# Reordering the edges between the stages of a two-block fp32 transformer program

## The chip, the cores and the metric

The program runs on one core of one Trainium2 chip. A core has four compute engines with their own instruction queues: TensorE (PE: matrix products into PSUM), VectorE (DVE), ScalarE (ACT) and GpSimd (POOL). SyncE (SP) issues DMA transfers. The engines meet only through semaphores. The metric is the device time of one execution in microseconds (us).

## The reference

Two transformer blocks one after the other, on 256 tokens of width 2048, in float32. Cut to what matters here:

```
# block 1
x = x + mixed(rms_norm(x, g_mix)) @ w_out      # 16 heads: 6 differential, 4 block, 6 dilated
x = x + cross_attention(rms_norm(x), rms_norm(mem))          # w_cq, w_ckv, w_co
x = x + (silu(conv(h @ w_up_g)) * (h @ w_up_u)) @ w_down     # h = rms_norm(x), width 5632
x = rms_norm(x, g_final)
# block 2
h = h + 0.5 * rmsnorm(swiglu(rmsnorm(h)))                    # ff1
o_attn = nsa_attention(...)                                  # 8 heads
log_a = -8 * sigmoid(xc @ w_a + b_a) * softplus(-lam); a = exp(log_a)
u = sqrt(1 - exp(2 * log_a)) * (sigmoid(xc @ w_i + b_i) * xc)
o_rec = scan(a, u) * gelu(yb)                                # h_t = a_t h_(t-1) + u_t
h = h + rmsnorm(concat(rmsnorm(o_attn), rmsnorm(o_rec)) @ w_out)
h = h + 0.5 * rmsnorm(swiglu(rmsnorm(h)))                    # ff2
h = h + rmsnorm(sigmoid(rmsnorm(h) @ w_ple_gate) * (p @ w_ple_proj))
```

## The kernel before

**Data and precision.** Activations lie transposed: 128 features on the partitions, 256 tokens along the free dimension, so width 2048 is 16 chunks. X holds the residual stream. Every float32 product is made of three faster ones. Weights and operands are split into a high part and a low part (value minus high part), and hi*hi, hi*lo and lo*hi are added in PSUM. OPR and HR hold operand chunks as (high, low) pairs.

**Units.** The weights (about 590 MB) stream once. SyncE loads a unit of 256 x 512 weights (512 KB) into one of four slots of `raw` (L450). ScalarE copies it to `wh` (`split`, L1061), VectorE subtracts to get `wl` (`split`, L1583), TensorE multiplies. `LEAD` is 4: each engine issues the split of unit n+4 at its place for unit n, and ScalarE's split waits until TensorE has used the slot. In `gemm` (TensorE, L575 on) a unit is 16 matmuls: for each of two chunks and four output tiles one of 512 columns (high weights times high and low operand, L610 or L615) and one of 256 (low weights times high operand, L612). In `unit` (L640 on; matmuls L648, L650, L651), used for w_in_b, w_out, nsa, wo_a and wo_r, it is 24 matmuls of 256 columns.

**Phases** run in the order of the list PHASES: w_in, w_in_b, w_out, w_ck, w_cq, w_cv, w_co, up, down, ff1_up, ff1_down, in_c, nsa, wo_a, wo_r, ff2_up, ff2_down, ple_gate, ple_p, ple_gb, ple_pl. A column block of 512 outputs takes 4 PSUM banks, and blocks alternate between the two halves of PSUM. At its end ScalarE copies the half of the sum that came from the low operand (`take`, L1079), VectorE adds the other (`collect`, L1597) and frees the banks (`acc_free`); `residual` then adds to X (L1690). In four phases (PAIRED: up, ff1_up, ff2_up, ple_gate) the first two column blocks run interleaved, so each pair of operand chunks serves two units.

**Norms.** Before a norm's first product the operand is the un-normalised x times the gain: ScalarE writes the high part (L1162), VectorE the low part (`prep`, L1754), chunk by chunk. The sum of squares is folded on VectorE (`fold`, L1709 to L1718), summed over partitions by TensorE with a matrix of ones (`stat` L538, `late_stat` L573, `post_stat` L561), rooted on ScalarE (`std`, L1147) and inverted on VectorE (`rstd`, L1725). The scale is applied at evacuation. Norms behind a phase (`post_stat`, `post_norm`) must be complete before the next one starts; `post_norm` then updates X (L1779 and L1781 for the single chunks 0 to 3, L1786 and L1791 for groups of four). Meanwhile TensorE runs filler matmuls whose result nobody reads (`keep_busy`, L548): 8 and then 20, none at ple_post.

**Order written by hand.** Each engine's program is a straight list of steps. In w_in_b and w_out 88 steps interleave units with the heads of attention: step s on TensorE is unit s and then pieces of heads. The unit order of w_out is OUT_UNITS, pairs of column block c and weight rows r; rows 3 and 4 need the four heads that finish last (head outputs L1875). In nsa 84 steps do the same with eight heads whose scores stand at steps 50, 54, ... 78 (NSTART), the rotary turns (TURNS_OF_ROPE, products L937, VectorE `rotate` L2141), and two units of recurrent gates, ("r", 0) and ("r", 1), at steps 75 and 77 (`gate_pairs`, L865 to L867). A gate unit has four pairs of PSUM tiles in three banks, so its fourth pair waits for ScalarE's first sigmoid (`gate_sigmoids`, L1435). The exponentials of a head are `n_exp` (L1408). The gate scaling is VectorE's L2277. The recurrence (`recurrence(n)` on VectorE, L2290 to L2306, and ScalarE's L1508 to L1519) is interleaved with the 16 units of wo_a: product ig*xc (L2290), exp, tanh, exp, sqrt, product (L2297), eight scans (L2301), product with gelu (L2306).

Two places in which an engine's order decides, of ScalarE from L1444 on:

```
for s in range(84):
    if s in (75, 77):
        gate_sigmoids((75, 77).index(s), (0, 1, 2))
    if s > 0:
        split(n0 + s + LEAD, 0)
```

and of TensorE's wait for two chunks per unit: `lambda u: pe.wait_ge(xs_lo, first + per_unit * (u + 1))`.

GpSimd does the sums of squares of the norms behind a phase and of mem, attn and rec (`squares`, L2445 to L2448), each norm in its order, and nothing else. At the end VectorE updates X in four groups of four chunks, and SyncE stores each group (L527).

## Time and profile before

| | us |
|---|---|
| median of 3 runs | 3328.53 (3327.95 to 3330.65) |
| the profiled execution | 3328.18 |
| its span, first to last instruction | 3325.9 |
| mean granted TensorE clock | 0.993 |
| bytes moved by DMA | 595.78 MB, 179 GB/s on average |

The profiled execution's own time is 2.3 us longer than its span. The table of a profile's busy times says how long each engine had an instruction at work. The table of waits says, for each line, how long the engine stood idle before it and which instruction of which engine came last before it went on. A window adds up busy times in a stretch and shows the clock granted to TensorE (1.00 is 2.4 GHz, 0.50 is 1.2 GHz). A timeline lists instructions in order: start, duration, engine, line, operation, output <- inputs, shapes, and in brackets the idle time before.

### The profile page before, as it was taken

How to read it: one execution, taken by the hardware profiler on the slowest of the kernel's cores; microseconds unless marked ns; L12 is line 12 of the kernel's file. 1: busy time of each engine (PE TensorE's matmuls, PEld its weight loads, DVE VectorE, ACT ScalarE, POOL GpSimd, SP SyncE). 2: the span in 40 equal slices, each digit the busy share in tenths (PEclk: the TensorE clock that was granted, in tenths of full speed). 3: DMA queues.
4: the chain of work that ended last, by engine and by line, in shares of the span. 5: the costliest groups of instructions: out<-in, count | busy, mean ns of one | idle time of the engine just before them, and what ended most of it. 6: DMA issues, size and time to landing. Idle time of an engine off the chain costs nothing.

```text
span 3325.9 us, 51311 instructions
## 1 busy us (share of the span) xinstructions
PE 3252.5 (98%) x19952; PEld 2889.8 (87%) x19952; DVE 2102.9 (63%) x2273; ACT 1581.0 (48%) x1886; POOL 91.0 (3%) x38
## 2 busy tenths in 40 slices
PE   8999999999999999999999998999999999999997
PEld 7999987888888888888888887998988888888886
DVE  6676676766665546665565547756886555555477
ACT  5445455554454435444444434445644444444353
POOL 0000200000000100000000000000010000000001
PEclk9999999999999999999999999999999999999998
DMA  7555555666666555656656564754456566565543
GB/s 254 178 153 168 168 177 152 184 189 190 188 180 196 187 190 161 193 181 194 187 184 194 185 191 136 216 152 121 159 159 196 183 191 187 178 200 184 193 159 126
DMA packets 321867, 595.78 MB, mean 179 GB/s; under 512 B 18276, under 2 KB 41988, under 8 KB 321732
## 3 DMA queue, kind: packets, MB, share of 16 engines
q1 hardware_dynamic: 313856, 587.27, 56.7%
q10 hardware_dynamic: 7876, 6.63, 0.6%
q8 instruction: 93, 1.52, 0.2%
q14 instruction: 42, 0.34, 0.0%
HBM read 591.70 MB, written 2.13 MB: 179 GB/s over the span
## 4 chain that ended last, share of the span: by engine, by line
PE 94%; DVE 3%; ACT 1%; issue 1%; POOL 0%; DMA 0%; ACTq 0%; DVEq 0%; POOLq 0%
PE acc L610 26%; PE acc L612 25%; PE acc L615 24%; PE acc L648 5%; PE acc L650 5%; PE acc L651 5%; DVE wl L1583 1%; ACT wh L1061 0%; DVE RSTD L1725 0%; DVE T L1786 0%; PE acc L561 0%; PE acc L665 0%; PE acc L844 0%; PE acc L845 0%; PE acc L846 0%
## 5 line engine op out<-in xcount | busy, mean ns | idle before, releaser
L1583 DVE TENSOR_TENSOR wl<-raw,wh 128x1024 fp32r<-128x1024 f32 x1112 | 1388.1, 1257 | 1037.0 <-ACT wh L1061 1035.9
L1061 ACT ACTIVATE wh<-raw 128x1024 fp32r<-128x1024 f32 x1112 | 1165.9, 1057 | 1319.4 <-PE acc L615 1047.3
L612 PEld LDWEIGHTS acc<-OPR,wl 128*128 128x128 f32 x4992 | 940.8, 188 | 207.2
L610 PE MATMUL acc<-OPR,wh 128*128 128x512 f32 x2658 | 1041.7, 397 | 17.9 <-DVE OPR L1754 11.8
L612 PE MATMUL acc<-OPR,wl 128*128 128x256 f32 x4992 | 1011.3, 279 | 0.0
L615 PE MATMUL acc<-OPR,wh 128*128 128x512 f32 x2334 | 924.6, 396 | 0.0
L610 PEld LDWEIGHTS acc<-OPR,wh 128*128 128x128 f32 x2658 | 505.9, 190 | 38.4 <-issue 10.2
L612 PEld LDWEIGHTS acc<-HR,wl 128*128 128x128 f32 x2208 | 414.9, 188 | 95.0
L610 PE MATMUL acc<-HR,wh 128*128 128x512 f32 x1138 | 447.1, 396 | 1.0 <-DVE HF L1597 1.0
L612 PE MATMUL acc<-HR,wl 128*128 128x256 f32 x2208 | 439.7, 278 | 0.0
L615 PEld LDWEIGHTS acc<-OPR,wh 128*128 128x128 f32 x2334 | 438.2, 188 | 0.0
L615 PE MATMUL acc<-HR,wh 128*128 128x512 f32 x1070 | 423.3, 396 | 0.0
L648 PE MATMUL acc<-OPR,wh 128*128 128x256 f32 x1216 | 350.4, 288 | 2.9 <-DVE wl L1583 2.9
L650 PE MATMUL acc<-OPR,wh 128*128 128x256 f32 x1216 | 344.5, 283 | 0.0
L651 PE MATMUL acc<-OPR,wl 128*128 128x256 f32 x1216 | 344.4, 283 | 0.0
L648 PEld LDWEIGHTS acc<-OPR,wh 128*128 128x128 f32 x1216 | 233.6, 192 | 8.1 <-issue 7.9
L650 PEld LDWEIGHTS acc<-OPR,wh 128*128 128x128 f32 x1216 | 233.7, 192 | 0.9 <-issue 0.7
L651 PEld LDWEIGHTS acc<-OPR,wl 128*128 128x128 f32 x1216 | 233.5, 192 | 0.0
L610 PEld LDWEIGHTS acc<-HR,wh 128*128 128x128 f32 x1138 | 215.9, 190 | 4.8 <-DVE HF L1597 1.6
L615 PEld LDWEIGHTS acc<-HR,wh 128*128 128x128 f32 x1070 | 200.5, 187 | 0.0
L1079 ACT ACTIVATE T<-acc 128x1024 f32<-128x1024 f32 x94 | 95.0, 1010 | 17.7 <-PE acc L615 16.3
L1597 DVE TENSOR_TENSOR T<-acc,T 128x1024 f32<-128x1024 f32 x78 | 95.1, 1219 | 1.0 <-ACT T L1079 1.0
(346 smaller groups left out, 2008.2 us busy)
## 6 DMA issues: line engine op xcount, KB each, us to landing
raw<-in_w_up SPq DMA_DIRECT2D x176, 512.0 KB, 4.4
raw<-in_ff_w_gate SPq DMA_DIRECT2D x176, 512.0 KB, 3.8
raw<-in_ff_w_up SPq DMA_DIRECT2D x176, 512.0 KB, 4.4
raw<-in_ff_w_down SPq DMA_DIRECT2D x176, 512.0 KB, 3.8
raw<-in_w_in SPq DMA_DIRECT2D x170, 512.0 KB, 3.9
raw<-in_w_down SPq DMA_DIRECT2D x88, 512.0 KB, 4.0
raw<-in_w_out SPq DMA_DIRECT2D x64, 512.0 KB, 3.8
raw<-in_w_ple_gate SPq DMA_DIRECT2D x32, 512.0 KB, 3.9
```

The costliest lines, as they stand in the source:

```text
L610: pe.matmul(acc[:, b + t, :], wh[:, s, col:col + P], x, start=first, stop=False)
L612: mm = pe.matmul(acc[:, b + t, 0:T], wl[:, s, col:col + P], x[:, 0, :], start=False, stop=last and t % 2 == 0)
L615: mm = pe.matmul(acc[:, b + t, :], wh[:, s, col:col + P], x, start=False, stop=last)
L648: pe.matmul(dst, w_hi, ks[k][:, 0, :], start=first and k == 0 and t % 2 == 0, stop=False, skip_group_check=True)
L650: pe.matmul(dst, w_hi, ks[k][:, 1, :], start=False, stop=False, skip_group_check=True)
L651: mm = pe.matmul(dst, w_lo, ks[k][:, 0, :], start=False, stop=last and k == 1, skip_group_check=True)
L1061: act.activation(wh[:, s, :], raw[:, s, :], ACT.Copy).then_inc(hi_done, 1)
L1079: act.activation(T1[:, 0:tiles, :], acc[:, b:b + tiles, T:2 * T], ACT.Copy).then_inc(t1_full, 1)
L1583: dve.tensor_tensor(wl[:, s, :], raw[:, s, :], wh[:, s, :].bitcast(F32), ALU.subtract)\
L1597: dve.tensor_tensor(dst, acc[:, b:b + tiles, 0:T], T1[:, 0:tiles, :], ALU.add).then_inc(acc_free, 1)
```

## The change

TensorE's program:
- The bias-table product (L634) moves behind unit 3 of w_in.
- In w_in the late statistic comes behind unit 2 of block 1, not unit 1.
- A paired phase waits for the last evacuation (`acc_free`) only at its second unit; in up, ff1_up, ff2_up and ple_gate its first unit waits chunk by chunk.
- In w_out the last units of blocks 0 and 1 are ordered rows 3, 3, 4, 4; rows 3 wait for 11 parts, not 13.
- TensorE waits for the root of the memory statistic behind w_out's last unit, not at once.
- One rotary turn moves from step 55 to 56. The recurrent gates move to steps 79 and 81. TensorE waits for the last sigmoid before wo_a. The attention statistic comes behind unit 2 of wo_a, not unit 3.
- At ple_post 12 filler matmuls run.

ScalarE and VectorE: the last split of w_cv moves behind the head outputs, the last split of w_co behind the residual. The updates of the first chunks are reordered around the operands. Gate scaling moves to steps 82 and 83. A small sigmoid stands ahead of the gates at step 79. The functions of the recurrence come one step earlier; A's exponential stands ahead of `std("attn")`. The product ig*xc goes from VectorE to GpSimd, behind the attention squares. At the end ScalarE multiplies the output by its gain into YG, the fold of ple_post comes earlier, and VectorE updates five groups (4, 4, 4, 2, 2 chunks), each stored by itself.

```diff
@@ lists
-             + [(0, 3), (0, 4), (1, 3), (1, 4)] + ...
+             + [(0, 3), (1, 3), (0, 4), (1, 4)] + ...
-    return units + rec[:25] + [("r", 0), rec[25], ("r", 1)] + rec[26:]
+    return units + rec[:29] + [("r", 0), rec[29], ("r", 1)] + rec[30:]
-TURNS_OF_ROPE = {..., 53: (5, 4, 7), 55: (6, 6, 7)}
+TURNS_OF_ROPE = {..., 53: (5, 4, 7), 56: (6, 6, 7)}
+OUT_GROUPS = [(0, 4), (4, 8), (8, 12), (12, 14), (14, 16)]
+        YG = HFc[:, 52:68, :]
@@ sync
-            for g in range(4):
-                sp.wait_ge(out_done, g + 1)
+            for n, (first, last) in enumerate(OUT_GROUPS):
+                sp.wait_ge(out_done, n + 1)
...
@@ tensor, post_stat
-                if name != "ple_post":
-                    keep_busy(name, 8)
+                keep_busy(name, 12 if name == "ple_post" else 8)
@@ tensor, gemm
-                    if paired:
-                        pe.wait_ge(acc_free, g)
-                    elif g >= 2:
+                    if g >= 2:
                         pe.wait_ge(acc_free, i * 2 + (g - 1))
...
-                        ready(u)
+                        if paired and v == 1:
+                            pe.wait_ge(acc_free, g)
+                        if half is None or v > 0 or not paired:
+                            ready(u)
                         pe.wait_ge(lo_done, i * (2 * ph["upc"]) + (n + 1))
                         for k in range(chunks):
+                            if half is not None and v == 0 and paired:
+                                pe.wait_ge(xs_lo, half + k + 1)
...
+                        if g == 0 and u == 3:
+                            pe.wait_ge(tab_loaded, 48)
+                            pe.matmul(acc[0:16, 2, :], HF[0:32, 0:16], HF[0:32, 512:1024], start=True, stop=True)\
+                              .then_inc(rt_ps, 1)
...
-                        if norm and isinstance(i, int) and c == late and u == 1:
+                        if norm and isinstance(i, int) and c == late and u == (2 if name == "w_in" else 1):
@@ tensor, w_out
-                first, last = s in (0, 6, 16, 24), s in (13, 15, 23, 31)
+                first, last = s in (0, 6, 16, 24), s in (14, 15, 23, 31)
-                pe.wait_ge(xs_lo, XS["attn1"] + (13 if r in (3, 4) else 9 if r >= 5 else 3))
+                pe.wait_ge(xs_lo, XS["attn1"] + (13 if r == 4 else 11 if r == 3 else 9 if r >= 5 else 3))
-                    stat("mem", colsum)
+                    stat("mem", colsum, wait=False)
+            pe.wait_ge(var_ready, N["mem"] + 1)
@@ tensor, wo_a
+            pe.wait_ge(r_sig, 8)
-                if n == 3:
+                if n == 2:
                     stat("attn", colsum, wait=False)
@@ scalar and vector, w_cv and w_co
-                split(PH["w_cv"]["u0"] + u + LEAD, 0)
+                if u < 7:
+                    split(PH["w_cv"]["u0"] + u + LEAD, 0)
...
+            split(PH["w_cv"]["u0"] + 7 + LEAD, 0)
-                splits(ph, c, 0)
+                splits(ph, c, 0, 0, 1 if c == 3 else 2)
...
+            splits(ph, 3, 0, 1)
@@ scalar, nsa and wo_a
-                if s in (75, 77):
-                    gate_sigmoids((75, 77).index(s), (0, 1, 2))
+                if s == 79:
+                    act.activation(SM[:, 62:63], SM[:, 60:61], ACT.Sigmoid)
+                if s in (79, 81):
+                    gate_sigmoids((79, 81).index(s), (0, 1, 2))
-                if n == 3:
-                    std("attn", 1024)
-                if n == 3:
+                if n == 2:
                     act.wait_ge(r_la, 1)
                     act.wait_ge(units_used, n0 + 84)
                     act.activation(A_, LA, ACT.Exp).then_inc(r_a, 1)
+                    std("attn", 1024)
...
@@ scalar, end
+            def scale_y(g):
+                act.wait_ge(y_done, g + 1)
+                for c in range(4 * g, 4 * g + 4):
+                    ins = act.activation(YG[:, c, :], HFc[:, 20 + c, :], ACT.Copy, scale=v("ple_post_g_2", c))
+                ins.then_inc(y_scaled, 1)
...
@@ vector, prep of the first chunks
                     if update and c == 0:
                         update(0, 0)
-                    if update and c < 3:
-                        update(0, c + 1)
+                        update(0, 1)
+                    elif update and c == 2:
+                        update(0, 3)
...
                     if c == 1 and sq in FIRST_X:
+                        update(0, 2)
                         split(ph["u0"] + 3, 0)
@@ vector, nsa and wo_a
-                if s in (80, 82):
+                if s in (82, 83):
...
-                if n == 2:
-                    dve.wait_ge(r_sig, 8)
-                    dve.tensor_tensor(IX, IX, XC, ALU.mult).then_inc(r_ix, 1)
-                if n == 5:
+                if n == 4:
                     dve.wait_ge(r_a, 3)
                     dve.scalar_tensor_tensor(LA, LA, 1.0, XC, ALU.add, ALU.mult).then_inc(r_w, 1)
-                if n == 7:
+                if n == 6:
...
-                if n in (8, 9):
+                for c in {7: (0, 1), 8: (2, 3, 4), 9: (5, 6, 7)}.get(n, ()):
...
@@ vector, end
+            early_fold("ple_post")
             collect(gb, 1, 0, gate(3))
             collected(gb, 1, 0)
             apply_rstd(3)
-            early_fold("ple_post")
...
+            for n, (first, last) in enumerate(OUT_GROUPS):
+                k = last - first
+                dve.wait_ge(y_scaled, first // 4 + 1)
+                if n >= 1:
+                    dve.wait_ge(out_done, n)
+                chain(dve.tensor_tensor(T2[:, 0:k, :], YG[:, first:last, :], bc(RSTD[:, :], k), ALU.mult))
+                dve.tensor_tensor(X[:, first:last, :], X[:, first:last, :], T2[:, 0:k, :], ALU.add).then_inc(out_done, 1)
@@ gpsimd
             squares("attn", four(HFc, OF, 1), n_of, 8, 0)
+            gp.wait_ge(r_sig, 8)
+            gp.wait_ge(xc_lo, 8)
+            gp.tensor_tensor(IX, IX, XC, ALU.mult).then_inc(r_ix, 1)
```

## Rows read from the trace of the kernel before

**Rows 1.** The page, first part: busy us (share of the span) xinstructions of each engine.

```profile
PE 3252.5 (98%) x19952; PEld 2889.8 (87%) x19952; DVE 2102.9 (63%) x2273; ACT 1581.0 (48%) x1886; POOL 91.0 (3%) x38
```

**Rows 2.** Waits of TensorE: line <- releaser: us in total, times, longest.

```profile
PE acc L610 <- DVE OPR L1754: 11.8, 7, 2.9
PE acc L634 <- DMA HF<-in_diag: 9.9, 1, 9.9
PE acc L865 <- ACT HF L1435: 4.9, 1, 4.9
PE acc L610 <- DVE T L1597: 4.4, 1, 4.4
PE acc L648 <- DVE wl L1583: 2.9, 3, 2.2
PE acc L573 <- issue: 2.9, 2, 2.3
PE acc L779 <- DVE HF L1979: 2.7, 1, 2.7
...
PE acc L648 <- ACT S L1147: 2.6, 1, 2.6
PE acc L648 <- DVE HR L1875: 2.4, 1, 2.4
...
PE acc L937 <- DVE S L2141: 1.4, 1, 1.4
```

**Rows 3.** Windows: length, busy us (x) of PE PEld DVE ACT POOL, PEclk, DMA.

```profile
363.50:366.90 3.40, 3.40 (x18) 3.40 (x18) 0.00 (x0) 0.04 (x1) 3.24 (x3) 0.50 0.39 136
407.90:411.30 3.40, 3.40 (x18) 3.40 (x17) 1.16 (x1) 0.00 (x0) 0.00 (x0) 0.50 0.47 149
532.60:537.60 5.00, 5.00 (x16) 4.32 (x17) 1.98 (x3) 0.19 (x1) 0.00 (x0) 0.50 0.31 103
600.00:650.00 50.00, 50.00 (x289) 43.58 (x288) 33.71 (x34) 25.43 (x28) 0.00 (x0) 1.00 0.69 210
2308.10:2312.50 4.40, 4.36 (x20) 4.36 (x21) 1.23 (x1) 3.24 (x7) 0.00 (x0) 0.50 0.00 0
2338.70:2353.40 14.70, 14.68 (x121) 14.46 (x120) 13.52 (x19) 6.22 (x9) 1.93 (x1) 1.00 0.45 147
```

**Rows 4.** Timeline of VectorE at the edge of w_co and up: start, us, instruction.

```profile
531.31 1.22 DVE L1597 TENSOR_TENSOR T<-acc,T 128x1024 f32<-128x1024 f32 x1
```

**Rows 5.** Timeline of VectorE at the start of ff2_up.

```profile
2449.16 0.48 DVE L1754 SCALAR_TENSOR_TENSOR OPR<-X,vec,OPR 128x256 fp32r<-128x256 f32 x1
...
2450.41 0.48 DVE L1754 SCALAR_TENSOR_TENSOR OPR<-X,vec,OPR 128x256 fp32r<-128x256 f32 x1
```

**Rows 6.** Timeline of VectorE and TensorE around the attention statistic in wo_a.

```profile
2348.82 1.23 DVE L1583 TENSOR_TENSOR wl<-raw,wh 128x1024 fp32r<-128x1024 f32 x1 [1.08 <-ACT wh L1061]
2349.96 1.22 DVE L1709 TENSOR_TENSOR T<-HF 128x1024 f32<-128x1024 f32 x1
...
2353.68 0.70 PE L538 MATMUL acc<-S,ones 128*128 128x256 f32 x2 [0.30 <-DVE S L1718]
```

**Rows 7.** Timeline of GpSimd and VectorE where both work, and the product that moves.

```profile
366.24 2.39 POOL L2448 TENSOR_TENSOR S<-S 128x1024 f32<-128x1024 f32 x1
...
367.95 1.76 DVE L1583 TENSOR_TENSOR wl<-raw,wh 128x1024 fp32r<-128x1024 f32 x1 [5.75 <-ACT wh L1061]
...
2354.68 2.28 DVE L2290 TENSOR_TENSOR HF<-HF 128x2048 f32<-128x2048 f32 x1
```

**Rows 8.** Timeline of ScalarE before the recurrent gates' first sigmoid.

```profile
2305.96 1.28 ACT L1435 ACT_TABLE_LOAD   x1
```

**Rows 9.** Timeline of TensorE and VectorE at the end of the program.

```profile
3305.08 3.34 PE L561 MATMUL acc<-S,ones 128*128 128x256 f32 x8 [1.42 <-ACT S L1114]
...
3319.65 1.67 DVE L1786 SCALAR_TENSOR_TENSOR T<-HF,vec,RSTD 128x256 f32<-128x256 f32 x4
3321.36 1.22 DVE L1791 TENSOR_TENSOR X<-X,T 128x1024 f32<-128x1024 f32 x1
```

81 lines of the change are left out of this document (44 added, 37 removed).

## The prediction

> **What bounds the kernel now.** I read four views, in this order. The page's first part shows TensorE busy for 98% of the span [rows 1], and nearly all of that is matrix work which the change leaves alone. A gain can come from only two things: time in which TensorE stands still, and time in which it works at its lower clock. So I then read the table of TensorE's waits [rows 2], which names each standstill and the instruction that ended it. Third, windows laid over the stretches behind the longer waits: the granted clock there is 0.50, which is 1.2 GHz in place of 2.4, and TensorE works on through them [rows 3]. Every us at half clock costs half a us. Last, timelines of VectorE, ScalarE and GpSimd around each edge, to see what is late next once a wait goes [rows 4 to 9].
>
> The waits shown sum to about 46 us. The last matmuls end at 3308.4 [rows 9], 17.5 before the end of the span. The four slow stretches shown cost half of 16.2, about 8. The page shows no other loss, so the change must be added up edge by edge. A unit of 16 matmuls takes 2.8 us (289 in 50), one of 24 takes 2.9 (120 in 14.7) [rows 3].
>
> **The change part by part.** Gains carry a minus sign.
>
> *Start.* The bias-table product (L634) leaves the head of TensorE's queue, where it waited 9.9 us for its DMA [rows 2]. The first unit then waits for its own split, ready at the same time, and runs its 1.8 us earlier, but at half clock. That is worth 0.9, and the product, at full clock by then, costs about 0.9 behind unit 3. Sum 0, between -1 and +0.5.
>
> *w_in, second column block.* TensorE waited 2.3 of the 2.9 us at L573 for the column sums [rows 2]. The statistic now comes one unit later, and a unit of 2.8 us fills the wait. The split of unit 13 has one unit less in hand; I estimate that half a us is left, and 0.8 would come back if it is late. **-2.3**.
>
> *w_out.* The units of rows 3 are done before those of rows 4, each waiting only for its own heads. The 2.4 us at L648 <- HR L1875 goes [rows 2], and with it the 3.4 us at half clock right behind [rows 3], worth 1.7. The evacuation of block 0 moves from step 14 to 15 and is needed one unit of 2.9 us later; it takes as long as other additions of its size, 1.2 [rows 4]. **-4.1**.
>
> *Statistic of the memory.* TensorE no longer waits for ScalarE's root at L648 <- S L1147, 2.6 us, and the 3.4 us at half clock behind it lose their cause [rows 2, 3]. The root still blocks ScalarE, but a split is due three units after its slot is free: 8.7, less 1.1 and 1.2 for its two halves, leaves 6. **-4.3**.
>
> *w_cv to w_co.* One split moves behind the value evacuation. The wait of 2.7 us [rows 2] was ended by VectorE, which did that split first. What is late next is ScalarE's own evacuation behind its last copy. I take half, with 0 and 2.7 as bounds. **-1.4**.
>
> *w_co to up.* One split moves behind the last residual, and the first unit of up no longer waits for the last evacuation, which reads other banks. The wait of 4.4 us goes [rows 2]. The second unit still needs that evacuation: a copy of 1.0 and an addition of 1.2 [rows 4], behind one split and two operand halves on a packed VectorE; I make that 3.1 us against a unit of 2.8, so 0.3 comes back. Of the slow stretch behind, 5 us were worked [rows 3], worth 2.5. **-6.6**.
>
> *Rope.* One rotation moves from step 55 to 56; the 1.4 us at L937 goes [rows 2]. **-1.4**.
>
> *Waits per chunk in ff1, ff2 and ple.* Seven waits at L610 <- OPR L1754 make 11.8 us [rows 2]. In ff2 the first two chunks were ready at 2449.64 and 2450.89, the ends of the two L1754 rows [rows 5]. Starting on the first saves 1.25, in ple as much. In ff1 I take 0.4, since there the filler matmuls outlast the first chunk. Three of the seven waits, in the column block in_c, are VectorE's pace: there the reordered updates only add a wait for ScalarE's copy, +0.3. Behind ple_gate VectorE's chain can follow only in part, +0.4. **-2.2**.
>
> *End.* The sums of squares are folded before the last collection, so VectorE is 1.1 us freer when it matters. Twelve filler matmuls keep TensorE going: the eight statistic matmuls took 3.34 us at half clock [rows 9] and would take about half. ScalarE's table load of 1.28 [rows 8] becomes the later partner, so I make the reciprocal 1.3 earlier, not 1.7. Then four times a multiplication of 1.67 (4 instructions) and an addition of 1.22 [rows 9] become five pairs of plain VectorE operations at 1.22 for four chunks [rows 4] and 0.7 for two (an estimate, a little over half): about 10.3 against 11.8. ScalarE's scaling of groups 0 and 1 fits between its splits (it is 48% busy [rows 1]), that of 2 and 3 beside the reciprocal; a group late would cost up to 1.7. The last store is half as large: -0.3. **-3.1**.
>
> These sum to **-25.4**.
>
> *The recurrent branch* is where I expect a loss.
> - The gates move from steps 75 and 77 to 79 and 81. TensorE's 4.9 us at L865 [rows 2] came because ScalarE, in order, first did the exponentials of the head of step 74, then a table load of 1.28 [rows 8], then the sigmoid. Step 79 stands just so behind the head of step 78. The new dummy sigmoid stands behind the exponentials too, so it hides nothing. The wait stays, and so do the 4.4 slow us behind it [rows 3]. **+0.2** for the dummy.
> - The attention statistic moves from unit 3 to unit 2 of wo_a, but VectorE's fold stays behind its split of unit 1, which waits for TensorE. The fold began at 2349.96, and the statistic of 2353.68 waited 0.30 for its end, behind unit 3 [rows 6]. Unit 2 ends a unit of 2.9 earlier. So TensorE waits 3.2 where it waited 0.3: **+2.9**.
> - The product of 2048 columns, 2.28 on VectorE [rows 7], goes to GpSimd, in just this stretch. GpSimd needed 2.39 for 1024 columns of two sources, and a split which VectorE began meanwhile took 1.76 and ended only after GpSimd did [rows 7]; the usual split takes 1.23 [rows 6]. So VectorE stands still for about 4.8. It has 1.08 idle before the fold [rows 6], and four gate scalings move in too (about 1 overlapped; at 0.48 each [rows 5] 1.9). Operand halves for units 1 and 2 and the fold come 4.6 later. **+4.6**.
> - Freed of that product and with scans one step earlier, VectorE no longer delays three splits at the end of wo_a, 2.9 us [rows 2]. **-2.9**.
> - The chain through ScalarE and the scans now starts later. Its last product, then the operands of wo_r and the second fold, come about 2.4 after TensorE wants them. **+2.4**.
> - A wait of nearly 4 us may lower the clock once more, 1.7; I take half. **+0.9**.
>
> Sum **+8.1**, between 0 (VectorE and GpSimd side by side, chain in time) and +13 (GpSimd a third slower, two slow stretches).
>
> On GpSimd the row shows a split held until the other engine was done [rows 7]. The Trainium skill says the same in "SBUF — State Buffer", section "Who interferes with whom": a VectorE instruction with two SBUF inputs contends with a GpSimd instruction that reads SBUF, and the later one blocks fully. By that rule the term is 4.6; if the two only shared the port it would be near 2.
>
> A table load takes 1.28 in the row, with the next activation right behind it [rows 8]. The Trainium skill, "ScalarE: Activation LUTs", section "What ACT_TABLE_LOAD costs", gives about 2.7 with a drain for a change of set. The change adds one such load in wo_a; by that figure my sum would be an estimated 1.4 higher.
>
> Total: -25.4 + 8.1 = -17.3. The profiled execution took 3328.18 (span 3325.9), 0.35 below the median of the three runs, so 3310.9 on its own terms and about **3311** as a median.
>
> **The rivals.**
> - *The recurrent branch costs nothing.* For it: GpSimd's spans are rough, and VectorE is freed where it was late. Against it: the fold's order, which no other engine can shorten. With the branch at +1.5 the time is 3304.5. Chance 0.21.
> - *The gate wait goes.* The step's surroundings differ (no convolution work near step 79), so ScalarE may be free before. Then 4.9 and 2.2 less: about 3304. Against it: ScalarE's order is written out. Chance 0.09.
> - *Freed time is lost again.* TensorE arrives sooner at places paced by VectorE or by loads, and a third to a half of the 18 us won before up comes back as new waits. For it: VectorE's operand halves already hold TensorE seven times [rows 2]. Against it: between w_in and down nearly all VectorE work starts on TensorE's signals. About 3319. Chance 0.12.
> - *Slower.* Place: the 32 units of wo_a and wo_r. New waits at units 1, 2 and the statistic keep the clock at 1.2 GHz, so each unit of 2.9 us takes 5.8. It makes the kernel slower by over 0.2% once 17.3 + 6.7 = 24 us are eaten, which is after 8 to 9 slow units; all 32 would give 3311 + 92, about 3400. Against it: no slow stretch in rows 3 outlasts 7 us, after waits up to 4.9. Chance 0.03.
>
> My own account has 0.55.
>
> **How the numbers follow.** 0.2% of this time is 6.7 us, about what a measurement can tell from no change. The forecast with the bounds of its unknown terms reaches from 3305 to 3319, the first two rivals lie at 3304, the third at 3319. The range 3302 to 3319.5 leaves out less than 2 in 10. Faster by over 0.2% means below 3321.9: 0.55, 0.21, 0.09 and most of 0.12, less something for what I have not seen, 0.92. Within 0.2%: 0.05. Slower: 0.03.
>
> **What would show each step right or wrong.** In the waits after: no rows for w_out, memory or rope, L573 down to about half a us, and the residual wait at up near 0.3. The wait at L865 still near 5 with a table load before it. A wait of 3 to 4 us at L538 behind VectorE's L1718 analogue, and waits at L648 on operand halves in the first two units of wo_a. VectorE splits or scalings of over 3 us beside a GpSimd product of about 4.8. Fewer slow stretches before 600 us. I am wrong if the statistic's wait is under 1, if VectorE runs on beside GpSimd, or if waits before up return elsewhere.

## The result, and the profile after

The changed kernel takes **3308.77 us** (median of 4 runs, 3308.55 to 3310.74). The kernel before took 3329.18 beside it (median of 4, 3327.95 to 3330.65). The ratio is 0.9944, with a 95% interval of 0.9931 to 0.9956: 18.6 us faster, 14.6 to 23.0 (the two medians as they stand are 20.4 apart). The forecast was 3311.0, with a range from 3302 to 3319.5. The spans of the two profiled executions are 3325.9 and 3306.7, so the traces have 19.2 us to account for.

The page's first part, of the kernel after:

```profile
PE 3250.7 (98%) x19964; PEld 2889.8 (87%) x19964; DVE 2105.9 (64%) x2263; ACT 1587.6 (48%) x1903; POOL 97.5 (3%) x39
```

TensorE's busy time fell by 1.8 us [rows 1]; the rest of the 19.2 is standstill and the tail behind the last matmul. TensorE's waits after, whole span (line <- what ended the wait: us in total, times, longest):

```profile
PE acc L616 <- DVE wl L1610: 11.8, 2, 10.0
PE acc L616 <- DVE OPR L1782: 6.9, 5, 2.8
PE acc L874 <- ACT HF L1448: 5.6, 2, 5.0
PE acc L542 <- DVE S L1745: 3.2, 1, 3.2
PE acc L656 <- DVE OPR L2252: 2.4, 1, 2.4
PE acc L542 <- issue: 1.6, 1, 1.6
...
PE acc L788 <- DVE HF L2009: 1.3, 1, 1.3
PE acc L576 <- issue: 1.1, 1, 1.1
```

Lines have moved: L616 is the L610 of before, L656 is L648, L874 is L865, L542 is L538, L788 is L779, L576 is L573, L1610 is the split L1583, L1782 is L1754, L1745 is L1718. Compare with [rows 2]. In the first row 10.0 us are the first unit's wait for its own split, where the bias-table product waited 9.9 before. Gone are the waits of w_out (2.4), of the memory's root (2.6), of the residual ahead of up (4.4, of which 0.3 is left) and of the rotation (1.4), and at the end of wo_a those for VectorE's splits (2.9). The waits for operand halves at a stage's start (L1754, now L1782) went from seven with 11.8 us to five with 6.9, all in in_c. New in wo_a and wo_r are the statistic (3.2), operand halves (2.4), 0.8 at the operands of wo_r and 1.6 at the second statistic. L576 shows 1.1, not the half a us that I had named as a sign; it is all in in_c. The gate wait stands as it was, 5.0, with 0.6 more in the second gate unit.

Both programs have the same 1112 splits on ScalarE, one for each weight unit, so the n-th split serves as a milestone. Its start, in us:

| up to split | what lies before it | before | after | difference | of this stretch | forecast |
|---|---|---|---|---|---|---|
| 61 | start, w_in | 185.63 | 183.46 | -2.17 | -2.2 | 0, -2.3 |
| 123 | w_out | 395.79 | 389.44 | -6.35 | -4.2 | -4.1 |
| 146 | memory | 465.96 | 455.30 | -10.66 | -4.3 | -4.3 |
| 160 | w_cv to w_co | 517.08 | 505.03 | -12.05 | -1.4 | -1.4 |
| 301 | w_co to up | 919.87 | 901.48 | -18.39 | -6.3 | -6.6 |
| 651 | ff1 | 1907.15 | 1888.08 | -19.07 | -0.7 | -0.4 |
| 751 | in_c | 2197.41 | 2177.57 | -19.84 | -0.8 | +0.3 |
| 816 | rope, recurrent branch | 2449.70 | 2436.39 | -13.31 | +6.5 | -1.4 + 8.1 |
| 1001 | ff2 | 2968.07 | 2953.42 | -14.65 | -1.3 | -1.25 |
| 1091 | ple_gate | 3229.72 | 3213.76 | -15.96 | -1.3 | -1.25 |
| 1112 | ple_gb | 3290.00 | 3273.98 | -16.02 | -0.1 | +0.4 |
| end of span | end | 3325.9 | 3306.7 | -19.2 | -3.2 | -3.1 |

The shape is the forecast one: about 21 us are won up to the gates, 7.9 are lost between them and the end of wo_r, and some 6 are won behind. Up to 600 us [rows 3] has three low-clock windows. The first two lines below are about the same microseconds of w_out after the change, the other three are the low-clock windows around the recurrent branch (length, busy us (x) of PE, PEld, DVE, ACT, POOL, then the granted clock):

```profile
363.00:366.90 3.90, 3.90 (x35) 3.90 (x34) 1.99 (x3) 1.56 (x2) 3.82 (x2) 1.00 0.44 140
407.00:411.30 4.30, 4.30 (x38) 4.30 (x37) 1.41 (x2) 2.12 (x2) 0.00 (x0) 1.00 0.54 161
2302.70:2306.10 3.40, 2.87 (x13) 2.87 (x14) 0.03 (x1) 3.06 (x8) 0.00 (x0) 0.50 0.00 1
2326.60:2330.00 3.40, 3.40 (x18) 3.40 (x18) 3.40 (x8) 0.00 (x0) 0.00 (x0) 0.50 0.10 25
2336.80:2340.20 3.40, 3.35 (x13) 3.18 (x14) 1.12 (x1) 2.93 (x3) 0.00 (x0) 0.50 0.32 100
```

No low-clock window is left between 16 and 600 us. Around the branch there are three of 3.4 us, where one of 6.8 stood.

### The profile page after: what moved, and what is told of

Its sections match the earlier page's. It is cut to its first block, busy times and chain, and to the rows that moved or that the text cites. A ratio compares the mean times of both kernels' runs of the same rounds, so it can differ in the third digit from the quotient of the medians.

```text
span 3306.7 us, 51352 instructions
## 1 busy us (share of the span) xinstructions
PE 3250.7 (98%) x19964; PEld 2889.8 (87%) x19964; DVE 2105.9 (64%) x2263; ACT 1587.6 (48%) x1903; POOL 97.5 (3%) x39
## 4 chain that ended last, share of the span: by engine, by line
PE 95%; DVE 3%; ACT 1%; issue 1%; POOL 0%; DMA 0%; ACTq 0%; DVEq 0%; POOLq 0%
PE acc L616 26%; PE acc L618 25%; PE acc L621 24%; PE acc L656 5%; PE acc L658 5%; PE acc L659 5%; DVE wl L1610 1%; PE acc L552 1%; ACT wh L1071 0%; PE acc L673 0%; DVE HF L2309 0%; PE acc L853 0%; PE acc L854 0%; PE acc L855 0%; PE acc L760 0%
## 5 line engine op out<-in xcount | busy, mean ns | idle before, releaser
L1610 DVE TENSOR_TENSOR wl<-raw,wh 128x1024 fp32r<-128x1024 f32 x1112 | 1385.0, 1255 | 1013.8 <-ACT wh L1071 1012.4
L616 PE MATMUL acc<-OPR,wh 128*128 128x512 f32 x2658 | 1040.5, 397 | 19.2 <-DVE wl L1610 11.8
L616 PEld LDWEIGHTS acc<-OPR,wh 128*128 128x128 f32 x2658 | 505.2, 190 | 38.4 <-issue 14.3
L616 PE MATMUL acc<-HR,wh 128*128 128x512 f32 x1138 | 447.1, 396 | 1.0 <-DVE HF L1624 1.0
L656 PE MATMUL acc<-OPR,wh 128*128 128x256 f32 x1216 | 351.6, 289 | 3.7 <-DVE OPR L2252 2.4
L656 PEld LDWEIGHTS acc<-OPR,wh 128*128 128x128 f32 x1216 | 234.5, 193 | 9.0 <-issue 5.4
L616 PEld LDWEIGHTS acc<-HR,wh 128*128 128x128 f32 x1138 | 215.9, 190 | 4.8 <-DVE HF L1624 1.6
L1371 ACT ACTIVATE HR<-T 128x1024 f32 (+1 forms) x33 | 35.0, 1061 | 127.3 <-DVE T L2082 122.5
```

The lines of the kernel that those rows point to most:

```text
L616: pe.matmul(acc[:, b + t, :], wh[:, s, col:col + P], x, start=first, stop=False)
L656: pe.matmul(dst, w_hi, ks[k][:, 0, :], start=first and k == 0 and t % 2 == 0, stop=False, skip_group_check=True)
L1371: act.activation(HR[:, bass.ds(i * 4 + 4 * j, 4), 0, :], T2[:, :, :], ACT.Copy).then_inc(hid_hi, 1)
L1610: dve.tensor_tensor(wl[:, s, :], raw[:, s, :], wh[:, s, :].bitcast(F32), ALU.subtract)\
```

## The experiments

Every kernel ran beside the kernel before on the same chip; the first four below share a chip, the next three and the one with early edges undone a second, the spread scans and the two on the clock a third, and the one with the old order of the updates ran on a fourth. Medians are of 4 to 7 runs. The repeats of one kernel lie within 1 to 4 us, and the stretch up to split 61, which has the same code in all of them, alone moves a span by 1 us (the difference there is -2.2 after, but -2.2 to -3.2 in the experiments). So where less than 2 us matter I compare the traces, milestone by milestone.

The milestones vary too, with the place and length of the slow stretches. The last three kernels below have the changed kernel's code between splits 751 and 816. It loses 6.5 there, and they lose 7.4 (no matmuls ahead of the last statistic), 6.7 (early edges undone) and 7.4 (old order of the updates). In the two with 7.4 the gate wait of 5.0 us is followed by 6.8 us at half clock in place of 3.4. So a difference of under 1 us in this stretch says nothing, unless the slow stretches are alike. The window of the first of the three:

```profile
2300.50:2307.30 6.80, 4.83 (x22) 4.83 (x23) 2.63 (x8) 5.16 (x11) 0.00 (x0) 0.50 0.18 60
```

### Is the branch the loss?

**Branch back.** Gates, product, statistic and the steps of the recurrence as before, all else as after.

```diff
-    return units + rec[:29] + [("r", 0), rec[29], ("r", 1)] + rec[30:]
+    return units + rec[:25] + [("r", 0), rec[25], ("r", 1)] + rec[26:]
-                if s == 79:
-                    act.activation(SM[:, 62:63], SM[:, 60:61], ACT.Sigmoid)
-                if s in (79, 81):
+                if s in (75, 77):
...
+                if n == 2:
+                    dve.wait_ge(r_sig, 8)
+                    dve.tensor_tensor(IX, IX, XC, ALU.mult).then_inc(r_ix, 1)
```

> The changed kernel with the whole recurrent branch as it was before: gates at steps 75 and 77, the product on VectorE in unit 2 of wo_a, the attention statistic behind unit 3, its root, exponentials, scans and products one step later. Everything else of the change stays. My theory, that the branch costs time: in the two traces the distance between the kernels shrinks from about 21.6 us (behind the rope) to 13.3 us (end of wo_r), so this kernel should come out 8.3 us under the changed one, near 3300.5. In its trace the wait at the gate matmuls is about 4.9 and the statistic of the attention waits 0.3 or a little more. Rival, that the distance shrinks because TensorE arrives earlier at places that VectorE or the loads pace, whatever the branch does: then this kernel stays within 2 us of 3308.8 and the same waits stand in wo_a.

Measured: 3300.79 us, ratio 0.9918 (0.9905 to 0.9932). TensorE's waits from 2280 to 2440 us:

```profile
PE acc L874 <- ACT HF L1447: 4.9, 1, 4.9
PE acc L656 <- DVE wl L1607: 2.9, 3, 2.2
PE acc L564 <- ACT S L1123: 0.5, 1, 0.5
PE acc L542 <- DVE S L1742: 0.3, 1, 0.3
```

These are the waits of before. Between splits 751 and 816 this kernel gains 1.0 (-20.9 and -21.9 against the kernel before) where the changed one loses 6.5. So the branch costs 7.5 us, or 8.3 when this kernel is set against the two that have 6.8 slow us behind the gates, as it has. The gain of 1.0 is smaller than the rotation's 1.4 because 3.4 us at half clock follow the wait of 2.2 here (at 2368.3); the kernel before has that wait, but not the stretch.

**Product on VectorE again**, alone:

```diff
-            gp.wait_ge(r_sig, 8)
-            gp.wait_ge(xc_lo, 8)
-            gp.tensor_tensor(IX, IX, XC, ALU.mult).then_inc(r_ix, 1)
@@ vector, recurrence
+                if n == 2:
+                    dve.wait_ge(r_sig, 8)
+                    dve.tensor_tensor(IX, IX, XC, ALU.mult).then_inc(r_ix, 1)
```

> The changed kernel with only the product of input gate and convolution (2048 columns) back on VectorE, in unit 2 of wo_a. My theory: the scaling of 256 columns that took 4.69 us beside GpSimd's product takes 0.34 again, so the operand halves of units 0 and 1 are in time and the wait of 2.4 us at the head of wo_a goes with its slow stretch (1.7), while the statistic, which still follows VectorE's fold behind the split of unit 1, goes on waiting 2.5 to 3.3 us. About 3304.7. Rival, the held VectorE was waiting anyway and nothing else was due: 3308.8, and the 2.4 us stay or turn up at the fold. Second rival, the product's 2.28 us on VectorE is missed later in wo_a: between 3307 and 3309.

Measured: 3306.99 us, ratio 0.9934 (0.9921 to 0.9948), span 3304.7. Between splits 751 and 816 it loses 4.7 where the changed kernel loses 6.5: 1.8 less. The timeline of GpSimd in the changed kernel, then that of VectorE there (start, duration):

```profile
2318.30 1.92 POOL L2481 TENSOR_TENSOR S<-HF 128x1024 f32<-128x1024 f32 x1 [368.45 <-ACT HF L1436]
2320.19 4.65 POOL L2501 TENSOR_TENSOR HF<-HF 128x2048 f32<-128x2048 f32 x1
```

```profile
2318.13 7.12 DVE L2309 TENSOR_SCALAR HF<-HF,SM 128x256 f32<-128x256 f32 x4
2325.17 0.87 DVE L2252 SCALAR_TENSOR_TENSOR OPR<-HF,vec,OPR 128x256 fp32r<-128x256 f32 x2
```

And VectorE with the product back:

```profile
2319.20 2.77 DVE L2309 TENSOR_SCALAR HF<-HF,SM 128x256 f32<-128x256 f32 x4
2321.89 0.87 DVE L2252 SCALAR_TENSOR_TENSOR OPR<-HF,vec,OPR 128x256 fp32r<-128x256 f32 x2
```

The same four scalings take 7.12 us beside the 4.65 us product and 2.77 without it; in both, one of the four takes 1.99 beside GpSimd's squares. The row at L656 <- L2252 (2.4) is gone, as expected, and the statistic still waits 3.2. The slow stretches did not get fewer: two of 3.4 turned into one of 6.8, and the one behind the gate wait, in code that both kernels share, is 6.8 here and 3.4 in the changed kernel. Against the two kernels where it is 6.8 as well, 2.7 are saved. So the mechanism is as I said, and its price here is 1.8 to 2.7, not 4.

**Statistic behind unit 3 again**, alone:

```diff
-                if n == 2:
+                if n == 3:
                     stat("attn", colsum, wait=False)
@@ scalar, behind the exponential of A in step 2
-                    std("attn", 1024)
                 if n == 3:
+                    std("attn", 1024)
@@ vector
-                if n == 3:
+                if n == 4:
                     rstd("attn")
```

> The changed kernel with only the attention statistic behind unit 3 of wo_a again, the root and the reciprocal one step later with it. My theory: the statistic's wait of 3.25 us falls to 0.3 or so, since a unit of 2.9 lies before it, and the 3.4 us at half clock behind it lose their cause (1.7): about 3304.5. Rival, VectorE is late as a whole in wo_a and the wait only moves to the next place that needs it (the end of the first column block, or the operands of wo_r): within 1 us of 3308.8.

Measured: 3307.89 us, ratio 0.9939 (0.9926 to 0.9953), span 3306.3. The rival holds. TensorE's waits in the same stretch:

```profile
PE acc L656 <- DVE HF L2346: 4.2, 1, 4.2
PE acc L656 <- DVE OPR L2252: 2.4, 1, 2.4
...
PE acc L542 <- DVE S L1745: 0.4, 1, 0.4
```

The statistic waits 0.4 in place of 3.2, and the evacuation of the first column block (L2346) 4.2 in place of 0.5. What holds it is seen in ScalarE's timeline and then VectorE's:

```profile
2339.23 1.28 ACT L1157 ACT_TABLE_LOAD   x1
2340.52 0.47 ACT L1157 ACTIVATE S<-acc,SM 128x256 f32<-128x256 f32 x1
2341.01 1.28 ACT L1525 ACT_TABLE_LOAD   x1
2342.31 1.92 ACT L1525 ACTIVATE HF<-HF 128x2048 f32<-128x2048 f32 x1
2344.26 1.92 ACT L1527 ACTIVATE HF<-HF 128x2048 f32<-128x2048 f32 x1
2346.08 1.99 ACT L1071 ACTIVATE wh<-raw 128x1024 fp32r<-128x1024 f32 x2
```

```profile
2347.15 1.23 DVE L1610 TENSOR_TENSOR wl<-raw,wh 128x1024 fp32r<-128x1024 f32 x1 [6.68 <-ACT wh L1071]
2348.29 1.75 DVE L1752 RECIPROCAL RSTD<-S 128x256 f32<-128x256 f32 x1
2350.07 2.29 DVE L2322 SCALAR_TENSOR_TENSOR HF<-HF 128x2048 f32<-128x2048 f32 x1
2352.28 1.22 DVE L2346 TENSOR_TENSOR HF<-acc,RSTD 128x1024 f32<-128x1024 f32 x1
```

ScalarE does the root and two functions of 2048 columns, with two table loads, before its next split. VectorE idles 6.68 us for that split, then does the reciprocal and the 2.29 us product of the recurrence, and only then the evacuation. One step earlier in the recurrence means ahead of the evacuation.

**First gates at step 77**, second at 81, no extra sigmoid:

```diff
-    return units + rec[:29] + [("r", 0), rec[29], ("r", 1)] + rec[30:]
+    return units + rec[:27] + [("r", 0)] + rec[27:30] + [("r", 1)] + rec[30:]
...
-                    gate_sigmoids((79, 81).index(s), (0, 1, 2))
+                    gate_sigmoids((77, 81).index(s), (0, 1, 2))
...
```

> The changed kernel with the first set of gate matmuls and its sigmoids at step 77, between the exponentials of the heads at steps 74 and 78, and the second set left at 81; the extra sigmoid that only loads the table is dropped. My theory: TensorE's 5.0 us in the first set come from ScalarE doing the exponentials of the head just before, and at step 77 ScalarE is free, so the wait goes to under 1 us and with it the slow stretch behind (1.7): 3302 to 3303. Rival, the wait is the price of the four banks and the sigmoids themselves wherever they stand: a wait of 3 us or more is left at the gate matmuls. Second rival, the 6 us are given back in wo_a, where VectorE and GpSimd then have less time: 3306 to 3308, with longer waits on operand halves.

Measured: 3304.97 us, ratio 0.9930 (0.9917 to 0.9944). The waits for the sigmoids fall from 5.6 to 3.3 in all (1.2 and 2.0), each behind a table load; no slow stretch follows them, and the rows of wo_a are those of the changed kernel. Between splits 751 and 816 the kernel loses 2.9 where the changed one loses 6.5: 3.7 less. The profile has a slow stretch of 3.4 at 580 us which neither kernel has (+1.6), and the one in in_c falls where nothing hides it (+1.0, more on that below), so its span, 3304.8, is high by 2.5. The median lies between my theory (3302 to 3303) and the second rival. The first rival, 3 us or more wherever the gates stand, fell: in the unit that moved, the wait went from 5.0 to 1.2. The wait was ScalarE's exponentials, less the loads.

### Which part of the branch?

**Only the gates moved**, and **the same with the product on GpSimd**. In both the statistic is behind unit 3 again and the recurrence one step later, as before the change; the first also has the product on VectorE. Against the changed kernel:

```diff
@@ scalar: exponential, tanh, root, gelu of the recurrence one step later; std("attn") ahead of the exponential
@@ vector, recurrence
-                if n == 4:
+                if n == 5:
                     dve.wait_ge(r_a, 3)
-                if n == 6:
+                if n == 7:
                     dve.wait_ge(r_sw, 1)
-                for c in {7: (0, 1), 8: (2, 3, 4), 9: (5, 6, 7)}.get(n, ()):
+                if n in (8, 9):
```

> Of the recurrent branch only the gates stay moved (steps 79 and 81, their scalings at 82 and 83, the extra sigmoid); the product is back on VectorE, the attention statistic behind unit 3, and the root, exponentials, scans and products one step later, as before the change. The kernel with the whole branch back took 3300.8. My theory now: what cost 7.5 us in the branch is not the place of the gates (their two waits are 5.0 and 0.6, against 4.9) but what was moved inside wo_a: the product (2.0 measured alone) and VectorE's product of 2048 columns one step earlier, ahead of the evacuation of the first column block, where it waits for ScalarE. So 3301.5, between 3300.5 and 3303, with no wait on the evacuation in wo_a. Rival, the late gates themselves push VectorE's fold and operand halves back: 3304 or more, with a wait of over 2 us at the head of wo_a or at the statistic.

Measured: 3302.23 us, ratio 0.9926 (0.9912 to 0.9939), span 3299.6 against 3298.1 with the branch back. The gate waits are 5.6, and the other rows are again those of before (2.9, 0.5, 0.3). Between splits 751 and 816 it is 1.2 us behind that run, with slow stretches of the same lengths behind the same waits: the price of the late gates.

> As the run with only the gates moved, but the product of 2048 columns stays on GpSimd. My theory: the same as that run plus the 2.4 us at the head of wo_a (operand halves behind the scaling that GpSimd holds up) and perhaps one slow stretch (1.7): 3304 to 3305.6, and the wait of 4.2 us on the evacuation of the first column block, which stood in the run with only the statistic moved back, is gone since VectorE's long product stands behind that evacuation again. Rival, that wait came from the held VectorE and not from the order: then it is still there at 4 us and the time is 3307 to 3309.

Measured: 3306.01 us, ratio 0.9937 (0.9923 to 0.9951), 3.8 over the run without GpSimd's product on the same chip. The waits:

```profile
PE acc L874 <- ACT HF L1448: 5.6, 2, 5.0
PE acc L656 <- DVE OPR L2252: 3.4, 2, 2.4
PE acc L656 <- DVE wl L1610: 2.6, 2, 2.2
PE acc L542 <- DVE S L1745: 0.6, 1, 0.6
```

No wait on the evacuation: it came from the order, not from the held VectorE. And with the recurrence at its old place the product on GpSimd costs 3.8 (4.1 between the splits, the slow stretches alike), more than the same edit is worth in the changed kernel (1.8 to 2.7). The parts of the branch don't add: taken back one by one they give 1.8 to 2.7 and 0.5, the gates cost 1.2, and all together are 7.5 to 8.3. That they fall due behind each other on the same VectorE is my reading of the waits; no run tests it by itself.

**Both gates between two heads.** The branch as before, gates at 77 and 78, the one-column sigmoid at 76:

```diff
+    return units + rec[:27] + [("r", 0), ("r", 1)] + rec[27:]
+                if s == 76:
+                    act.activation(SM[:, 62:63], SM[:, 60:61], ACT.Sigmoid)
+                if s in (77, 78):
+                    gate_sigmoids((77, 78).index(s), (0, 1, 2))
```

> All of the branch as before the change, but the two gate units stand at steps 77 and 78, both between the exponentials of the heads at 74 and 78, and a one-column sigmoid at step 76 loads the table ahead of them; scalings at 80 and 82. My theory: the 4.9 us at the gates and the slow stretch of 6.8 behind it (3.4) go, since ScalarE is idle there: 3300.8 - 8 = 3293, and 1 us more if the fourth pair of each unit still waits for a sigmoid: 3292.5 to 3294.5. Rival, the second unit directly behind the first needs four banks that are not yet read, and the exponentials at 78 come late behind eight sigmoids: waits of 3 us are left and the time is 3296 to 3298.

Measured: **3296.67 us**, ratio 0.9908 (0.9893 to 0.9924), 12 under the changed kernel. The waits, then ScalarE's timeline there:

```profile
PE acc L656 <- DVE wl L1610: 2.9, 3, 2.2
PE acc L874 <- ACT HF L1448: 1.9, 2, 1.2
```

```profile
2285.50 1.28 ACT L1459 ACT_TABLE_LOAD   x1
2286.79 0.20 ACT L1459 ACTIVATE SM<-SM 128x1 f32<-128x1 f32 x1
2286.90 1.04 ACT L1071 ACTIVATE wh<-raw 128x1024 fp32r<-128x1024 f32 x1
2287.85 2.28 ACT L1448 ACTIVATE HF<-acc,vec 128x256 f32<-128x256 f32 x6
```

Between splits 751 and 816 it gains 5.5 us, the run with the branch back 1.0: 4.6 for the gates, where I expected 8. The time is the rival's (3296 to 3298), though 1.9 us of waits are left, not 3. Waits make 3.0 of the 4.6. The load starts at 2285.5, when TensorE is already at the gate unit, because ScalarE did the exponentials of step 74 and a split until then; so the load isn't hidden, and 1.2 of the first wait stays. And I had booked 3.4 for the slow stretch of 6.8. In the run with the branch back its window reads:

```profile
2283.00:2289.70 6.70, 3.89 (x18) 3.89 (x19) 2.72 (x9) 5.96 (x14) 0.00 (x0) 0.50 0.27 78
```

TensorE is busy for 3.89 of the 6.70 us; the rest is the wait itself. So the half clock cost at most half of 3.89, 1.9 and not 3.4; the 4.6 less the 3.0 of waits leave 1.6.

**Spreading the scans** on top of it:

```diff
-                if n in (8, 9):
-                    for c in range(4 * (n - 8), 4 * (n - 8) + 4):
+                for c in {7: (0, 1), 8: (2, 3, 4), 9: (5, 6, 7)}.get(n, ()):
```

> The kernel with the gates at steps 77 and 78 (3296.7), and from the change inside wo_a only the spreading: two scans in step 7, three each in 8 and 9, and the last product in two halves in steps 10 and 11; everything else in wo_a at its place of before. My theory: VectorE has 0.8 us idle behind its product in step 7, so two scans there cost nothing and take 1.3 us out of steps 8 and 9; the waits for VectorE's splits at the end of wo_a (0.36, 0.36, 2.2) fall to 1 us or less in all, and the slow stretch of 3.4 behind them (1.7) may go: 3293.5, between 3292.5 and 3296. Rival, the operands of wo_r, which need the last product, become the wait instead, now 1 us at the head of wo_r: 3296 to 3298.

Measured: **3296.12 us**, ratio 0.9902 (0.9887 to 0.9917), span 0.6 less than the run before it. VectorE's splits are in time (2.9 to 0.6), but 1.7 and 1.6 us turn up at the operands of wo_r and its statistic, which the changed kernel has too (0.8 and 1.6). The slow stretch behind them is gone. So the rival holds: the wait moved to wo_r. This is the fastest version I have: it beats the kernel before by some 33 us and the changed one by 12.6, but not measurably the one without the spreading.

### The clock

**A wait filled with matmuls.** The changed kernel, and ahead of the attention statistic:

```diff
                 if n == 2:
+                    for _ in range(13):
+                        pe.matmul(acc[:, 7, :], OPR[:, 8, 0, 0:P], OPR[:, 8, :, :], start=True, stop=True)
                     stat("attn", colsum, wait=False)
```

> The changed kernel with 13 matmuls of 512 columns, whose result nobody reads, ahead of the attention statistic, in the place where TensorE waits 3.25 us for VectorE's fold. At 0.23 us each they take 3.0. My theory, that a slow stretch follows a standstill: the wait shrinks to about 0.3 and the 3.4 us at half clock that follow it are not there, which is worth 1.7: 3307.1, with one slow stretch in wo_a (behind the operand halves) instead of two. Rival, the clock goes down for another reason than the standstill itself: the stretch is still there and the time is 3308.8 or a little more.

Measured: 3307.80 us, ratio 0.9938 (0.9924 to 0.9952), span 3305.0, 1.7 less. The wait at L542 is 0.3, and the window that stood at 0.50 now reads:

```profile
2336.80:2340.20 3.40, 3.40 (x28) 3.35 (x29) 0.94 (x1) 2.76 (x3) 0.00 (x0) 1.00 0.34 108
```

28 matmuls in place of 13. The slow stretch followed from the standstill: filled, it is gone, and between splits 751 and 816 that is worth 1.5, a little under half the stretch's length.

**No matmuls ahead of the last statistic:**

```diff
-                keep_busy(name, 12 if name == "ple_post" else 8)
+                if name != "ple_post":
+                    keep_busy(name, 8)
```

> The changed kernel without the twelve matmuls that keep TensorE busy ahead of the last statistic. My theory: TensorE stands still for 3 us or more behind the last column block, the eight statistic matmuls run at half clock again and take 3.3 us in place of 2.4, and everything behind them comes 0.8 to 1.5 us later: 3309.6 to 3310.3. Rival, the eight are paced by ScalarE's squares and its table load, which ends 0.1 us after them: under 0.5 us, not to be seen in the time.

Measured: 3309.45 us, ratio 0.9942 (0.9928 to 0.9955), span 3307.2. The eight statistic matmuls after, and in this run:

```profile
3288.62 2.40 PE L564 MATMUL acc<-S,ones 128*128 128x256 f32 x8 [0.37 <-ACT S L1124]
```

```profile
3288.63 2.93 PE L565 MATMUL acc<-S,ones 128*128 128x256 f32 x8 [3.14 <-ACT S L1125]
```

0.53 more, of which the span shows 0.5: nearly the rival. The last four wait for ScalarE's second square, and ScalarE's table load ends only 0.1 behind the eight in the changed kernel.

### The edges before and behind

**Early edges undone** in the changed kernel: w_out's order, the memory's root, and whole units again in up, ff1, ff2 and ple_gate:

```diff
-             + [(0, 3), (1, 3), (0, 4), (1, 4)] + ...
+             + [(0, 3), (0, 4), (1, 3), (1, 4)] + ...
-                    stat("mem", colsum, wait=False)
-            pe.wait_ge(var_ready, N["mem"] + 1)
+                    stat("mem", colsum)
-            gemm("up", *from_op(XS["ffn"]), half=XS["ffn"], norm="ffn")
+            gemm("up", *from_op(XS["ffn"]), norm="ffn")
...
```

> The changed kernel with five early edges undone: the order of w_out's units and the step of its first evacuation, the wait for the memory's root, and the waits per chunk in up, ff1, ff2 and ple_gate (whole units again). My theory, that the edges add up one by one as in the traces: w_out +4.2, memory +4.3, up +1.2 (one operand pair), ff1 +0.7, ff2 +1.3, ple +1.3, together +13: 3321.8. The waits of 2.4 and 2.6 us and two slow stretches of 3.4 stand before 450 us again. Rival, the edges hide one another (a wait taken away at one edge comes back at the next, since the same engines are behind): less than 9 us, under 3318.

Measured: 3318.37 us, ratio 0.9972 (0.9961 to 0.9983): 9.6 over the changed kernel where I expected 13 and the rival, edges that hide one another, under 9. By the milestones w_out loses 2.7 (expected 4.2), the memory 4.3 (4.3), up 1.6 (1.2), ff1 0.3 (0.7), ff2 and ple 0.7 each (1.3). Two windows tell the first (both lie right behind a wait, of 2.4 and of 2.6 us):

```profile
359.60:363.00 3.40, 3.40 (x28) 3.40 (x29) 0.00 (x0) 0.21 (x1) 3.32 (x2) 1.00 0.51 154
403.30:406.70 3.40, 3.40 (x17) 3.40 (x18) 1.56 (x1) 0.00 (x0) 0.00 (x0) 0.50 0.46 154
```

The wait of 2.4 in w_out is back, but this time no slow stretch follows it. And the 1.6 at up is a slow stretch at 587.6 us; the wait for the operands there is the same 0.31 as after, so starting on the first chunk gained nothing at up. The shortfall is no hiding: 1.5 is the stretch that did not come in w_out, and ff2 and ple kept half of their gain without the waits per chunk, which I can't explain.

**VectorE's updates in the old order**, at the four edges:

```diff
                     if update and c == 0:
                         update(0, 0)
-                        update(0, 1)
-                    elif update and c == 2:
-                        update(0, 3)
+                    if update and c < 3:
+                        update(0, c + 1)
...
-                        update(0, 2)
```

> The changed kernel with the order of VectorE's updates at the four stage edges as before: the second update ahead of the second operand half instead of ahead of the first, the third and fourth ahead of the third. The waits per chunk stay. My theory: the new order, which I had priced as a cost of 0.3 in the column block in_c, is what gave 1.0 there (8.9 us of waits before, 8.0 after, with nothing else changed), and about half of the 1.3 at ff2 and at ple, since the kernel with whole units kept the other half. Put back it costs 1.0 in in_c, 0.6 at ff2 and at ple and 0.3 at ff1: 3311.3, from 3310 to 3312. Rival, the gain in in_c is a by-product of where TensorE arrives, and the order matters nowhere: 3308.8, with 8.0 us of waits in in_c.

Measured: 3308.27 us, ratio 0.9940 (0.9926 to 0.9954). No loss: the rival on the time holds, and my theory of in_c was wrong. Through in_c (splits 651 to 751) this kernel gains 1.05, the changed one 0.77. Its slow stretch in in_c begins at 2027.1, and the run with only the gates moved, which has the new order and a stretch from 2027.2, gains 0.77 too. So the new order costs 0.28 there. What gives the gain is the place of the slow stretch. TensorE's waits from 2000 to 2060 us, of the changed kernel and of the run with the statistic behind unit 3, which are the same kernel up to there:

```profile
PE acc L616 <- DVE OPR L1782: 6.9, 5, 2.8
PE acc L576 <- issue: 1.1, 1, 1.1
```

```profile
PE acc L616 <- DVE OPR L1782: 8.5, 5, 2.8
PE acc L576 <- issue: 0.6, 1, 0.6
```

In the first the 3.4 us at half clock begin at 2029.6, before the last wait for VectorE, and that wait shrinks from 2.8 to 1.3. In the second they begin at 2036.9, behind the last wait, where nothing hides them (as before the change, at 2056.5). The first kind gains 0.8 in in_c, the second loses 0.3.

## Why the prediction was right, step by step

The time came out 2.2 us under the forecast, and the account behind it, gains of 25 and a loss of 8 in the branch, is what the traces show: 27.1 and 7.9. Within the branch the sum is right and its terms are not.

- **Start and w_in, w_out, memory, w_cv to w_co, up, rope.** -20.1 forecast with the rope's 1.4, -19.8 measured. All terms hold to 0.3. One was right by luck: w_out's 1.7 for the slow stretch. The kernel with the early edges undone had the wait without the stretch. So w_out is worth 2.7 to 4.2. For the memory the stretch came back with the wait.
- **Waits per chunk.** -2.2 forecast, -4.2 measured, and that is the whole miss. The +0.3 in in_c was right (0.28), but a slow stretch fell where VectorE sets the pace, -1.05. (Of the seven waits four, 8.4 us, were in in_c, not three as I read it.) The +0.4 behind ple_gate did not come: the two waits in ple_gb are 0.2 and 0.8 before and after. ff1 gave 0.7 for 0.4. At ff2 and ple 1.3 each were right, though with whole units half of it was there too (0.6 each), so the chunk waits are worth 0.7.
- **End.** -3.1 forecast, -3.2 measured. The reciprocal starts 1.3 us earlier against the last split (the figure of the step). VectorE's ten operations take 10.7 from the first start to the last end, forecast 10.3, before 11.8. What follows the last of them is 0.8 shorter (3.3 to 2.6), forecast 0.3. The filler matmuls give 0.5 of it.
- **The branch.** +8.1 forecast, +7.9 in the trace, 7.5 to 8.3 by the kernel with the branch back. By its terms it is less good. The gates cost 1.2, not 0.2: the second gate unit waits 0.6 and the first the 0.1 of the dummy more, and TensorE works 4.55 of the 6.7 slow us in place of 3.89, which is 0.3. The product costs 1.8 to 2.7 with the rest of the branch in place and 3.8 without, not 4.6; the wait that it puts on operand halves is 2.4. The splits' 2.9 went, and the late chain put 0.8 and 1.6 on, as forecast. ScalarE has one table load more in wo_a, as forecast, and one fewer ahead of it, each of 1.28 with the next activation right behind, so the estimated 1.4 for a dearer load was not needed. The statistic's +2.9 is in the waits (3.2 for 0.3), but it is no cost of its own: taken away, it came back as 4.2 at the evacuation. In its place stands what I had booked as a gain, the recurrence one step earlier: VectorE's product of 2.29 us now lies ahead of the evacuation, and with the statistic behind unit 3 ScalarE's two functions lie ahead of the split that VectorE does before reciprocal and evacuation. My reading is that all of these are one lateness of VectorE and ScalarE, seen at different places, and that which term carries it depends on which is undone first. That the sum came within 0.2 is luck in part: the same code lost 0.8 more in two other runs.
- **VectorE beside GpSimd.** VectorE was blocked as forecast, though the instruction held was not one with two tensors from SBUF: a scaling of one tensor by a value per partition, which began 0.1 us behind GpSimd's product, took 4.69 us in place of 0.34 and ended 0.15 us behind it. The Trainium skill, "SBUF — State Buffer", section "Who interferes with whom", says that issue order decides who blocks, and that `tensor_scalar` may take the ports shared with GpSimd too; the trace agrees (four scalings in 7.12 us in place of 2.77).
- **The rivals.** "The branch costs nothing" and "the gate wait goes" fell: 5.0 us stood, behind the same exponentials. Gates at 77 show that the second could have been had in large part, with another step. "Freed time is lost again" fell up to the gates, where every edge kept its gain. The slower case had no slow stretch over 7 us before the last matmuls to feed it.

What stays open: why one standstill of 2.4 us is followed by a slow stretch and the same one in the next kernel is not. The Trainium skill, "TensorE: Matmul & The Clock Gate", section "What's actually happening", says of the start of a kernel that how many matmuls run at the lower clock differs between runs of the same kernel, with the moment at which they fall. The standstills here would fit that, but the page does not speak of them there, and no run sets that moment on purpose.

## What to carry to other kernels

Add a change up edge by edge, but within one stage treat the waits as one chain: a wait that is taken away from the statistic may only have kept another, at the evacuation, from being seen. Place a function of a shared in-order engine by what stands ahead of it there (a head's exponentials, a table load), not by the step number alone; gates two and three steps earlier, between two heads, were worth 5.6 us (3302.2 to 3296.7 on one chip). Don't move an elementwise product to GpSimd in a stage where VectorE has work due: here it cost 1.8 to 3.8 us. And before a difference of 1 us is put down to an edit, lay the slow stretches of the two traces side by side.

## What the runs showed of the hardware that I had not expected

- A slow stretch of 3.4 us costs 1.5 to 1.6 where TensorE sets the pace (the filled wait, and up in two runs). In in_c, in front of a wait for VectorE, it cost nothing: the wait shrank by 1.6 (2.8 to 1.3).
- A standstill of 2.4 to 5 us is often followed by one or two such stretches, but not always: in w_out the clock fell in one kernel and not in the other, and behind the gate wait of 5.0 us the stretch is 3.4 long in the changed kernel and 6.8 in the one with the product on VectorE, which is the same code up to there. Filling 3 us of the statistic's wait with matmuls took away the stretch behind that wait.
- GpSimd's product of 2048 columns with two sources takes 4.65 us, while a scaling on VectorE stands still; VectorE needs 2.28 for the same product [rows 7].
